# Recurrent stage: nine of a tile's 31 convolution taps in other places of VectorE's order, and the key root's inverse two taps later

## The reference, cut to what matters

```python
# recurrence, per head of 64 features (16 heads), over 512 positions
S = S * w_t + (S @ -kk_t) (kk_t * a_t)^T + v_t k_t^T ;  o_t = S r_t
kk = kk / max(norm(kk), 1e-12)              # per head and position
# convolution over the positions, 1024 channels, each with its own 31 taps
u = glu_in[..., :1024] * sigmoid(glu_in[..., 1024:])
u = conv(u, conv_w, width 31, causal, feature_group_count=1024) + conv_b
```

## Time and profile before

| | |
|---|---|
| median of 3 executions | 2215.86 us (2214.8 to 2217.65) |
| the profiled execution | 2215.59 us |
| its span in the profile | 2213.8 us |
| granted TensorE clock, mean over the span | 0.971 |
| busy: TensorE matmul, VectorE, ScalarE, GpSimd | 2081.9, 1154.8, 785.2, 731.0 us |
| recurrent stage, tiles 0 to 7 | about 1006 to 1627 us of the span |
| one tile of the stage | 77.8 us |

### The profile page before, as it was taken

One profiled execution on the slowest core, in us unless ns is written; L12 is line 12 of the kernel. 1 busy time (PEld: TensorE's weight loads), 2 busy tenths in 40 slices (PEclk: granted clock), 3 DMA queues, 4 the chain that ended last, 5 costly groups with the idle time before them and its releaser, 6 DMA issues. The chain is left out here.

```text
span 2213.8 us, 35978 instructions
## 1 busy us (share of the span) xinstructions
PE 2081.9 (94%) x14896; PEld 1645.4 (74%) x14896; DVE 1154.8 (52%) x1803; ACT 785.2 (35%) x1292; POOL 731.0 (33%) x347
## 2 busy tenths in 40 slices
PE   5898889999899999989999999999999998999997
PEld 5785566788688888767767777776777787888886
DVE  6426776333552432746677778667723457524322
ACT  2335656223332332442334333333334434323221
POOL 0321020434344444352332233233223343444442
PEclk9979999999899999989999999999999999999998
DMA  7541011543133333331111111111123332333331
GB/s 263 181 136 45 30 47 38 178 133 102 60 101 97 95 95 97 101 107 32 40 47 37 37 40 47 35 40 44 44 66 121 115 97 75 96 97 103 96 95 67
DMA packets 52465, 186.88 MB, mean 84 GB/s; under 512 B 5840, under 2 KB 6992, under 8 KB 51920
## 3 DMA queue, kind: packets, MB, share of 16 engines
q1 hardware_dynamic: 48528, 174.49, 25.3%
q10 hardware_dynamic: 3776, 10.09, 1.3%
HBM read 178.27 MB, written 6.29 MB: 83 GB/s over the span
## 5 line engine op out<-in xcount | busy, mean ns | idle before, releaser
L682 POOL TENSOR_TENSOR wlo<-raw,whi 128x1024 fp32r<-128x1024 f32 x266 | 643.7, 2420 | 1314.5 <-ACT whi L1298 1314.5
L765 PE MATMUL psum<-ah,whi 128*128 128x512 f32 x1288 | 540.7, 420 | 28.8 <-POOL wlo L682 16.9
L766 PE MATMUL psum<-ah,whi 128*128 128x512 f32 x1288 | 514.2, 399 | 0.0
L767 PE MATMUL psum<-ah,wlo 128*128 128x512 f32 x1288 | 512.9, 398 | 0.0
L1298 ACT ACTIVATE whi<-raw 128x1024 fp32r<-128x1024 f32 x266 | 280.1, 1053 | 358.0 <-PE psum L767 292.6
L765 PEld LDWEIGHTS psum<-ah,whi 128*128 128x128 f32 x1288 | 248.3, 193 | 102.5 <-POOL wlo L682 27.3
L767 PEld LDWEIGHTS psum<-ah,wlo 128*128 128x128 f32 x1288 | 248.6, 193 | 54.9
L766 PEld LDWEIGHTS psum<-ah,whi 128*128 128x128 f32 x1288 | 249.3, 194 | 43.4 <-issue 0.2
L2008 DVE SCALAR_TENSOR_TENSOR x<-upad,vec,x 128x512 f32<-128x512 f32 x240 | 210.7, 878 | 5.1
L765 PE MATMUL psum<-hidden,whi 128*128 128x512 f32 x536 | 209.8, 392 | 0.1
L766 PE MATMUL psum<-hidden,whi 128*128 128x512 f32 x536 | 209.5, 391 | 0.0
(11 more groups left out here) (340 smaller groups left out, 2850.5 us busy)
## 6 DMA issues: line engine op xcount, KB each, us to landing
raw<-in_w SPq DMA_DIRECT2D x322, 512.0 KB, 3.6
x<-in_x SPq DMA_DIRECT2D x1, 2048.0 KB, 8.1
x_kept<-x ACTq DMA_DIRECT2D x1, 2048.0 KB, 9.5
ao_kept<-ao ACTq DMA_DIRECT2D x8, 256.0 KB, 2.2
aof<-ao_kept ACTq DMA_DIRECT2D x1, 2048.0 KB, 10.8
x<-x_kept ACTq DMA_DIRECT2D x1, 2048.0 KB, 9.2
out<-x SPq DMA_DIRECT2D x8, 256.0 KB, 2.5
lwt<-in_lw ACTq DMA_DIRECT2D x8, 128.0 KB, 2.1
```

Of the source, the lines that this page charges most:

```text
L682: pool.tensor_tensor(wlo[:, s % NHL, :], raw_of(SPLITS[s]), whi[:, s % NHL, :].bitcast(F32), ALU.subtract).then_inc(lo_done, 1)
L765: pe.matmul(dst, wh, h_, start=first, stop=False)
L766: pe.matmul(dst, wh, l_, start=False, stop=False)
L767: return pe.matmul(dst, wl, h_, start=False, stop=last)
```

## The change

The taps of a slot come from a list with one entry per slot. Eight taps leave five slots (two each from the slots behind `ip` of level 1, behind `inv` of level 2 and behind `ip` of level 4, one each from the slot behind `ip` of level 5 and the slot behind `tav`), and the 31st tap leaves the end of the tile. Two taps now stand at the head of the tile, two behind the reciprocal of the group norm of the tile before (ahead of `akv`), two more in the slot behind `rr`, and three behind `pt`. The reciprocal of `kkss` becomes a step of its own, `kkinv`, and goes behind the two taps of its slot.

```diff
-            + v[2:3] + [("lg2", j)] + v[3:] + [("kkss", j)] + g[:1] + [("mix", j, 2)] + g[1:2] + [("kkb", j)] + g[2:3] + [("bonus", j)]
+            + v[2:3] + [("lg2", j)] + v[3:] + [("kkss", j), ("kkinv", j)] + g[:1] + [("mix", j, 2)] + g[1:2] + [("kkb", j)] + g[2:3] + [("bonus", j)]
...
+TAPS = (0, 2, 2, 2, 2, 0, 2, 2, 2, 0, 2, 2, 1, 2, 0, 3)
...
-        def slot(taps):
+        taps = list(TAPS)
+
+        def slot():
 
             got = [ahead.pop(0)] if ahead else []
-            while ahead and ahead[0][0] != "part":
+            while ahead and ahead[0][0] not in ("part", "kkinv"):
                 got.append(ahead.pop(0))
-            return got + [("conv", j, taps)]
-
-        out += [("tok", j, 0), ("mb", j, 0), ("tok", j, 1), ("mb", j, 1), ("iy0", j, 0), ("iy0", j, 1)]
+            got.append(("conv", j, taps.pop(0)))
+            return got + ([ahead.pop(0)] if ahead and ahead[0][0] == "kkinv" else [])
+
+        out += [("conv", j, 2), ("tok", j, 0), ("mb", j, 0), ("tok", j, 1), ("mb", j, 1), ("iy0", j, 0), ("iy0", j, 1)]
...
-        out += [("akv", j, 0), ("akv", j, 1), ("inv", j, 1, 0), ("opv", j)]
+        out += [("conv", j, 2), ("akv", j, 0), ("akv", j, 1), ("inv", j, 1, 0), ("opv", j)]
...
-        out += [("tav", j, 0), ("tav", j, 1)] + slot(1) + [("rr", j)] + slot(1)
-        out += [("opa", j)] + last[:1] + [("pt", j, 0), ("pt", j, 1)] + last[1:2] + [("qq", j, 0), ("qq", j, 1)]
+        out += [("tav", j, 0), ("tav", j, 1)] + slot() + [("rr", j)] + slot()
+        out += [("opa", j)] + last[:1] + [("pt", j, 0), ("pt", j, 1), ("conv", j, 3)] + last[1:2] + [("qq", j, 0), ("qq", j, 1)]
...
                     emptied_by(dve.tensor_scalar(nrt[:, :], bank(f)[:, 0:2 * TT], KK_EPS * KK_EPS, None, ALU.max), f)
+                elif kind == "kkinv":
                     dve.wait_ge(kkroot_done, j + 1)
                     dve.reciprocal(nrt[:, :], nrt[:, :]).then_inc(nrm_ready, 1)
```

More of the change, by code:

```diff
@@ L147, in first_tile @@
             + [("xn", 0), ("scale", 1, 0), ("hidden", 0)] + last1 + [("xput", 0)] + [("lw2", 0), ("la2", 0)] + own1 + [("scan", 0), ("hidden", 1), ("kk", 0)]
-            + v + [("lg2", 0), ("kkss", 0), ("mix", 0, 2)] + g1 + [("kkb", 0)] + g0 + [("bonus", 0), ("at", 0), ("re", 0)])
+            + v + [("lg2", 0), ("kkss", 0), ("kkinv", 0), ("mix", 0, 2)] + g1 + [("kkb", 0)] + g0 + [("bonus", 0), ("at", 0), ("re", 0)])
+TAPS = (0, 2, 2, 2, 2, 0, 2, 2, 2, 0, 2, 2, 1, 2, 0, 3)
 def rwkv_order():
@@ L176, in rwkv_order @@
                 out += [("gnb", j - 1), ("gnend", j - 1)]
-            out += slot(2)
-            out += [("iy", j, 0, lv), ("iy", j, 1, lv)] + slot(2)
+            out += slot()
+            out += [("iy", j, 0, lv), ("iy", j, 1, lv)] + slot()
             if lv == 2 and j:
@@ L181, in rwkv_order @@
             if lv < LEVELS:
-                out += [("inv", j, 0, lv), ("inv", j, 1, lv)] + slot(2)
-        out += [("tav", j, 0), ("tav", j, 1)] + slot(1) + [("rr", j)] + slot(1)
-        out += [("opa", j)] + last[:1] + [("pt", j, 0), ("pt", j, 1)] + last[1:2] + [("qq", j, 0), ("qq", j, 1)]
+                out += [("inv", j, 0, lv), ("inv", j, 1, lv)] + slot()
+        out += [("tav", j, 0), ("tav", j, 1)] + slot() + [("rr", j)] + slot()
+        out += [("opa", j)] + last[:1] + [("pt", j, 0), ("pt", j, 1), ("conv", j, 3)] + last[1:2] + [("qq", j, 0), ("qq", j, 1)]
         out += ahead + ([("re", j + 1)] if j + 1 < KT else [])
```

## The result

The changed kernel is slower by half a per cent: 2224.53 us median of nine runs (2218.41 to 2237.78) against 2215.26 of nine runs of the kernel before, ratio 1.0046 with a 95% interval of 1.0025 to 1.0066. The profiled execution took 2221.66 us, its span is 2219.9. In the changed file the lines behind the diff lie lower: by six, and by seven from VectorE's `kkinv` on.

What follows compares the result with a forecast made beforehand. TensorE was taken as the bound, busy 74.7 of 77.8 us a tile. From 2215.6 us, minus 17.2 for removed waits, plus 12.1 for the new wait and 11.6 for the clock, gave 2222.1 us, range 2205 to 2237.

Steps and rivals of the forecast that it cites:

- The prize: TensorE's waits for VectorE's `ip` and `iy` in tiles 0 to 6 would vanish: 12.2 + 5.0 = 17.2 us gained.
- The third wait: At `kkss`, reciprocal behind the taps: `ip` of level 5 starts 1.25 us earlier, removing TensorE's 1.1 us wait.
- The covers: Two added taps, up to 1.56 us, fit VectorE's idle: 1.62 at tile head, 1.82 behind group norm, 1.83 behind `rr`.
- The wait behind `pt`: GpSimd holds the three taps, so the state's chain waits for `st`: 1.73 us a tile, 12.1 over seven.
- The clock: Behind the chain's new wait, the clock falls in half of seven chains: 3.5 times 3.3 us, 11.6 us.
- The sum: Whole kernel: 2210.5 us with gain and new wait, 2222.1 us once the clock's falls are added.
- Rival 1: The chain's new wait comes but the clock holds: 2210.5 us, 2205 to 2213; chance 0.27.
- rival 2: The taps behind `pt` cost nothing, the 2.76 us idle being real cover: 2198.4 us; chance 0.13.
- Rival 3: Clock falls in every chain, recovering as slowly as at tile 0: 7 x 5.0 = 35 us, 2245.5; chance 0.07.

Runs made afterwards that it cites:

- experiment 1: Changed kernel without its three taps behind `pt` (two moved behind `iy` of level 3, the 31st to the tile's end): 2195.4 us, ratio 0.9923 to the kernel before.
- experiment 5: Kernel before with only the reciprocal of `kkss` put behind the two taps of its slot: 2209.21 us, ratio 0.9986.
- experiment 6: Kernel before with the reciprocal behind its taps and one level 5 tap moved to level 3's second slot: 2202.42 us, ratio 0.9957.
- experiment 2: Changed kernel with GpSimd's `wlo` issued later, which only put it behind `arow`, still meeting the first tap behind `pt`: 2208.96 us, ratio 0.9974 to the kernel before.
- experiment 7: Changed kernel with two taps behind `pt` instead of three, the 31st back at the tile's end: 2206.22 us, ratio 0.9955 to the kernel before.
- experiment 3: Changed kernel with GpSimd's `wlo` made to wait for the end of the state's chain, three taps kept behind `pt`: 2193.6 us, ratio 0.9913 to the kernel before.
- experiment 4: Kernel before with only three taps put behind `pt`, two from level 1's first slot and the 31st: 2242.37 us, ratio 1.0139.
- experiment 8: Changed kernel with two parts (six large matmuls) between the state's first and second steps, none behind the last: 2207.29 us, ratio 0.996 to the kernel before.

## Why the prediction was right

- **The prize, 17.2 us.** The waits fell by just that, and experiment 1 puts 2.61 us on the tile: 18.8 us over tiles 0 to 6 (547.1 against 528.3), with the longer waits of tiles 0 and 6. The sum was 1.6 us short. Ends of matmuls are modelled, so idle time is not the whole of what a wait costs: TensorE's busy time fell too, from 74.72 to 74.46 us a tile.
- **The third wait.** Right, and shown alone in experiments 5 and 6. I had not weighed that the pair of taps in level 5 would have run into `wlo`; I noted only that the remaining one ends early enough. The tap taken from there was part of the gain.
- **The covers** at the head, behind the group norm and behind `rr` held. TensorE has no new wait at any of them, and VectorE still stands idle for 0.40, 0.48 and 0.65 us there.
- **The wait behind `pt`.** The mechanism was as forecast, tap by tap: 2.60, 1.55 and 0.75 us against 2.5, 1.7 and 0.75. The size, 1.73 us, was measured as 1.44 to 1.50 (the second matmuls of the chain come 2.67 us behind the first instead of 1.17). The taps took 4.97 us where my chain made 5.0; the term was high by 0.2 to 0.3, most of it because the add came 0.23 us behind the last tap and not 0.40. Seven times, 10.1 to 10.5 us, not 12.1.
- **The clock.** Right in kind. I took 3.5 falls at 3.3 us; there were six at about 3.1 us in the profiled execution. The number of falls was the weakest figure, argued from one idle stretch of 1.51 us that kept the clock and those of 1.86 and 2.26 that lost it. Experiments 2 and 7 show falls behind 0.65 and 0.79 us: the length of one idle stretch was the wrong measure, and with 0.56 us idle just ahead and three large matmuls between, falls came behind far less. Nor do hold as a threshold, as the head of tile 0 below shows.
- **The sum.** 2222.1 against 2224.5 measured, or 6.5 us forecast against 9.3 between the medians. The sign comes from the mechanism, but that the total is so close is in part luck. Three of its errors offset one another: gain 1.6 too small, wait 1.6 to 2 too large, clock some 7 too small. With the gain and the wait as measured and the clock as forecast, the kernels would have come out some 3 us apart. Rival 1 failed on the clock, rival 2 on the three taps; without GpSimd's work beside them (experiment 3) rival 2 is just what happens. Rival 3 asked for seven falls at 5.0 us; where there were seven (experiment 4) they cost 2.6 each.

By the Trainium skill (TensorE: Matmul & The Clock Gate, "HAM oscillation — how this bites in real kernels") idle stretches of this length should not lower the clock. The runs go against it where several short ones stand close together, and the measurement decides. The Trainium skill also says (GPSIMD Engine Reference, "8. Key points") that GpSimd shares its SBUF interfaces with VectorE, so that instructions of VectorE with two SBUF inputs contend with it; the trace agrees, with 4.97 against 2.32 us for the same three taps.

What stays open: why tile 1 of the changed kernel kept its clock behind the same wait of 1.45 us (the large matmuls behind it still start 0.23 us apart), and so how many falls an execution has. The head of tile 0 asks the same question. In all ten profiles TensorE stands idle there for 2.26 or 2.27 us, waiting for VectorE's `arow`. In six the clock is at half for some 10 us behind it; in experiments 3, 5, 6 and 7 it stayed at 1.00 there. Experiment 1 and experiment 3, the first matmuls and then the tile:

```profile
1001.90 1.09 PE L1145 MATMUL psum<-eye_ones,arow 128*128 128x128 f32 x4 [2.27 <-DVE arow L2111]
1001.90:1079.16 77.26, 76.38 (x972) 57.82 (x972) 55.26 (x91) 24.05 (x39) 22.73 (x14) 0.94 0.13 37
```

```profile
1003.64 0.63 PE L1150 MATMUL psum<-eye_ones,arow 128*128 128x128 f32 x4 [2.27 <-DVE arow L2116]
1003.64:1076.98 73.34, 71.90 (x973) 54.07 (x973) 56.08 (x91) 23.97 (x39) 22.09 (x14) 1.00 0.11 32
```

The difference is 3.9 us, and nothing in the two kernels' order at this place accounts for it. So an idle stretch that lowers the clock in one execution can leave it alone in another. The nine runs of the changed kernel spread over 19 us, those of experiment 4 over 5 (2240.69 to 2245.34).

## What to carry to other kernels

An idle stretch in an engine's row is cover only for work that can really run in it: look at what the other engines do in that very moment, and count a VectorE instruction like these taps, with both operands in SBUF, as held until the GpSimd instruction beside it is done. A wait that is put into TensorE's dependent chain may cost more through the clock than through itself (here 1.5 and 2.6 us a tile), so put large matmuls next to it (experiment 8 did so), or move the work to a place where TensorE waits for nobody. And a hole that is filled upstream moves everything behind it: the taps of level 5 became harmful only when the reciprocal was out of the way.

## What the runs showed of the hardware that I had not expected

- A TensorE stage that idles 2.0 us more a tile in two pieces kept 2.4 GHz behind all seven chains (experiment 8), and one that idles 0.65 or 0.79 us more in one piece lost it in three or four of seven (experiments 2 and 7). The main difference was three more large matmuls ahead of the idle stretch.
- The same idle stretch of 2.27 us, at the head of tile 0, was followed by half clock in six profiled executions and by full clock in four.
- An engine that waits its turn behind the other can be helped by order alone: `arow` ahead of `wlo` (experiment 2) cut the three held taps from 4.97 to 3.84 us with the same work on both engines.
